# Where the product that spreads a norm's factor stands in three feed-forward layers

## The reference, cut to what matters

```python
D_FF = 2816

def rms_norm_2(x, g, eps=NORM_EPS):
    x32 = x.astype(jnp.float32)
    y = x32 * lax.rsqrt(jnp.mean(x32 * x32, axis=-1, keepdims=True) + eps)
    return (y * g.astype(jnp.float32)).astype(x.dtype)

def swiglu(h, w_gate, w_up, w_down):
    return (jax.nn.silu(h @ w_gate) * (h @ w_up)) @ w_down

for layer in range(DEPTH):          # DEPTH = 2
    x = x + 0.5 * swiglu(rms_norm_2(x, ffn_norm[layer, 0]), ...)
    ...                             # attention mixer, or RWKV time mixing
    x = x + 0.5 * swiglu(rms_norm_2(x, ffn_norm[layer, 1]), ...)
```

## Time and profile before

| | |
|---|---|
| median of 3 runs | 2799.5 us (2792.75 to 2800.39) |
| the profiled execution's own time | 2794.96 us |
| its span, from the first to the last instruction | 2793.2 us |
| mean granted TensorE clock | 0.947 |
| busy share of TensorE, DVE, ACT, POOL | 86%, 67%, 43%, 23% |
| spreading products start at (layers 1 to 4) | 1641.4, 1952.8, 2144.1, 2612.1 us |

### The profile page before, as it was taken

One profiled execution on the slowest core, in us unless ns is written; L12 is line 12 of the kernel. 1 busy time (PEld: TensorE's weight loads), 2 busy tenths in 40 slices (PEclk: granted clock), 3 DMA queues, 4 the chain that ended last, 5 costly groups with the idle time before them and its releaser, 6 DMA issues. The chain is left out here.

```text
span 2793.2 us, 35053 instructions
## 1 busy us (share of the span) xinstructions
PE 2397.1 (86%) x12802; PEld 1590.6 (57%) x12802; DVE 1861.0 (67%) x3446; ACT 1206.1 (43%) x2554; POOL 638.9 (23%) x530
## 2 busy tenths in 40 slices
PE   6987788888778887888888879998999997976999
PEld 5664333333224443433332268898888886865887
DVE  4667766677656757777765566676666665778665
ACT  3433434444335443444434354456445443534443
POOL 0003434554344433455544300000000000010000
PEclk8999999999999998999999999999999998966999
DMA  9789999999999888999999935542554554212553
GB/s 379 261 344 395 403 425 423 425 427 423 427 426 359 358 369 363 423 427 427 427 423 427 397 128 189 182 150 110 178 191 168 187 189 141 82 48 94 179 180 120
DMA packets 124203, 815.14 MB, mean 292 GB/s; under 512 B 15539, under 2 KB 20699, under 8 KB 29340
## 3 DMA queue, kind: packets, MB, share of 16 engines
q0 software_dynamic: 74016, 539.00, 46.2%
q1 hardware_dynamic: 50044, 274.27, 27.2%
HBM read 811.02 MB, written 1.15 MB: 291 GB/s over the span
## 5 line engine op out<-in xcount | busy, mean ns | idle before, releaser
L1372 PE MATMUL bank<-rows,diag 128*128 128x512 f32 (+1 forms) x2056 | 1018.3, 630 | 249.5 <-ACT diag L1522 246.6
L1754 DVE CUSTOM_DVE_ANT_0 rows<-rows,h 128x1024 f32<-128x1024 f32 (+1 forms) x512 | 622.3, 1225 | 399.4 <-DMA rows<-in_peer_rows,idx 395.9
L1372 PEld LDWEIGHTS bank<-rows,diag 128*128 128x128 f32 (+1 forms) x2056 | 374.6, 197 | 800.5 <-ACT diag L1522 482.1
L1259 POOL DMA_INDIRECT rows<-in_peer_rows,idx x512 | 618.9, 1209 | 777.2 <-PE bank L1372 651.4
L2091 PE MATMUL bank<-hT_pair,high 128*128 128x512 f32 x1408 | 503.2, 401 | 12.5 <-DVE work L2195 4.2
L2028 DVE TENSOR_TENSOR low<-weight_ring,high 128x2048 fp32r<-128x2048 f32 x148 | 338.4, 2289 | 164.8 <-ACT high L2023 164.8
L1513 ACT ACTIVATE picks<-picks 128x1 f32<-128x1 f32 (+1 forms) x512 | 103.4, 202 | 714.8 <-DVE picks L1754 710.2
L2092 PE MATMUL bank<-hT_pair,low 128*128 128x256 f32 x1408 | 396.1, 281 | 0.0
L2023 ACT CAST high<-weight_ring 128x2048 fp32r<-128x2048 f32 x148 | 281.8, 1908 | 147.7 <-PE bank L2100 115.8
L2091 PEld LDWEIGHTS bank<-hT_pair,high 128*128 128x128 f32 x1408 | 266.2, 189 | 81.0 <-issue 6.6
L2092 PEld LDWEIGHTS bank<-hT_pair,low 128*128 128x128 f32 x1408 | 267.5, 190 | 1.7
(11 more groups left out here) (540 smaller groups left out, 3265.5 us busy)
## 6 DMA issues: line engine op xcount, KB each, us to landing
weight_ring<-in_ffn_w_gate SPq DMA_DIRECT2D x44, 1024.0 KB, 4.8
weight_ring<-in_ffn_w_up SPq DMA_DIRECT2D x44, 1024.0 KB, 4.9
weight_ring<-in_ffn_w_down SPq DMA_DIRECT2D x44, 1024.0 KB, 4.8
mod_ring<-in_mod_w SPq DMA_DIRECT2D x16, 1024.0 KB, 7.1
weight_ring<-in_peer_w_q SPq DMA_DIRECT2D x16, 1024.0 KB, 12.2
half_ring<-in_mod_w SPq DMA_DIRECT2D x24, 512.0 KB, 7.9
rows<-in_mod_w SPq DMA_DIRECT2D x12, 1024.0 KB, 10.1
weight_ring<-in_attn_w_in SPq DMA_DIRECT2D x12, 1024.0 KB, 4.9
```

Of the source, the lines that this page charges most:

```text
L1259: nc.gpsimd.indirect_dma_start(ring[:, s], None, dram["peer_rows"], bass.IndirectOffsetOnAxis(ap=idx[:, T, n:n + 1], axis=0)).then_inc(row ...
L1372: mm = nc.tensor.matmul(bank[:, :], diag[0:n, j % DIAG_SLOTS], ring[0:n, j % ROW_SLOTS, D + half * 512:D + (half + 1) * 512], start=(j in ...
L1754: dotted.up(nc.vector.tensor_tensor_reduce(out=ring[r, s, 0:D], in0=ring[r, s, 0:D], in1=its_h, scale=1.0, scalar=0.0, op0=ALU.mult, op1=A ...
```

## The change

In the three layers whose first banks are the upper ones, TensorE goes on to piece 1's gate product right after piece 0, then makes the spreading product, then piece 1's up product. Piece 1's gate product no longer waits for a join, since banks 0 and 1 hold nothing then. The second layer stays as it was. No instruction is added on any engine.

```diff
@@ __init__
+        self.apart = not set(first_banks) & set(range(4))
@@ up_products
-    def up_products(self, pe, f, reg=None, late=None):
+    def up_products(self, pe, f, reg=None, late=None, which=(0, 1)):
-        for v in range(2):
+        for v in which:
             b = self.up_block(f, v)
             self.wait(pe, self.split.sem, self.p0 + b + 1, reg, 6)
-            if f > 0:
+            if f > 1 or f == 1 and (v == 1 or not self.apart):
                 self.wait(pe, self.steps.sem, self.m0 + 4 * (f - 1) + v + 1, reg, 8)
@@ multiply
+        def spread_factors():
+            pe.wait_ge(self.placed.sem, self.pl0 + 1)
+            for T in range(NT):
+                mm = nc.tensor.matmul(kit.bank[self.spread_bank][:, T * P:(T + 1) * P], kit.ones[:, 0:P], self.halves.spread[:, T, :],
+                                      start=True, stop=True)
+            mm.then_inc(self.spread.sem, 1)
+
         self.up_products(pe, 0, late=late)
-        pe.wait_ge(self.placed.sem, self.pl0 + 1)
-        ...
-        for f in (1, 2):
-            self.up_products(pe, f)
-            self.down_products(pe, f - 1)
+        if self.apart:
+            self.up_products(pe, 1, which=(0,))
+            spread_factors()
+            self.up_products(pe, 1, which=(1,))
+        else:
+            spread_factors()
+            self.up_products(pe, 1)
+        self.down_products(pe, 0)
+        self.up_products(pe, 2)
+        self.down_products(pe, 1)
```

More of the change, by code:

```diff
@@ L2114, in multiply @@
         kit, nc = self.kit, self.kit.nc
-        self.up_products(pe, 0, late=late)
-        pe.wait_ge(self.placed.sem, self.pl0 + 1)
[L2117 to L2120, removed]
-        for f in (1, 2):
-            self.up_products(pe, f)
-            self.down_products(pe, f - 1)
+        def spread_factors():
[4 more added lines that the diff above has]
+            mm.then_inc(self.spread.sem, 1)
+        self.up_products(pe, 0, late=late)
+        if self.apart:
[8 more added lines that the diff above has]
+        self.down_products(pe, 1)
         with pe.Fori(0, self.loops - 1) as i:
```

## The result

| | before | changed |
|---|---|---|
| median | 2792.82 us (6 runs) | 2813.77 us (6 runs, 2810.57 to 2816.11) |
| ratio | | 1.0068, 95% interval 1.0058 to 1.0078 |
| profiled execution, span | 2793.2 us | 2808.8 us |
| gate and up products wait for DVE L2028: total, times, longest | 4.2 us, 4, 1.2 | 26.8 us, 5, 8.2 |

The change costs 0.68%: 19.0 us on 2793, with an interval of 16.2 to 21.8 us. I had predicted 2817 us in a range of 2808 to 2824. The medians lie 21 us apart; the ratio, taken over all runs, gives less, since two of the six runs of the kernel before came out near 2800. The 25 and 23 further runs of the kernel before that were taken beside the experiments have medians of 2795.4 and 2795.45 us, 18 us under the changed kernel's.

The account below looks back on a forecast made before the run. TensorE was taken to bound the steady part, leaving only the layers' openings open to the change; 5.65 + 5.65 + 2.5 + 6.0 = 19.8 us on a mean of 2796.9 us gave 2817 us, range 2808 to 2824 us.

Parts of the forecast that it names:

- The chain is rigid: Fourth layer: the 8.13 us from the factor's copy to block 3's low part move whole with the later spreading product.
- Fourth and third layer +5.65 us each, first layer +2.5 us: Before piece 1's up: 16 gate pairs put ahead cost 5.65 us; in the first layer they partly fill the 2.66 us factor wait.
- Second layer 0: Opening of the second layer: order unchanged, so 0 us.
- The clock, 2.0 us a layer, 6.0 in all: Piece 1's up in three layers: slow pairs after 8.3 us of new idle time, 2.0 us each.
- its bounds of 4.2 and 9.6: Ends of the clock term over three layers: 3 x 1.4 = 4.2 us and 3 x 3.2 = 9.6 us.
- The lower row: First layer's gate of piece 1 before the change: five pairs take 3.23 us against 1.84, a loss of 1.4 us.
- leaving the term out: Sum without the slow clock, 13.8 us; as the rival where the clock stays up, 2811 us, 14%.
- The margin behind it: Piece 2's gate, waiting for block 5's split: 2.8 us of margin remain, so nothing more is lost or won back.
- The sum: Whole kernel: 5.65 + 5.65 + 2.5 + 6.0 = 19.8 us, added to a mean of 2796.9 us, predicting 2817 us.
- The faster rival: Piece 1's gate: idle time is filled and nothing comes late, 8.3 us won, time 2789 us; 2%.

Follow-up runs that it names:

- no_join_wait: Kernel before, with only the join's wait before piece 1's gate dropped in three layers, the spreading product staying ahead of that gate; ratio 1.0002 (0.9987 to 1.0017).
- early_block: Changed kernel, with block 3 (piece 1's up weights) split before piece 0 is treated, in all four layers; ratio 1.0029 (1.0018 to 1.0039).
- half_gate: Changed kernel, with the spreading product in the middle of piece 1's gate, behind 8 of its 16 pairs; ratio 1.0053 (1.0035 to 1.0072).

## Why the prediction was right

By its own steps:

- *The chain is rigid, 8.13 us from the copy to the split block.* Right to the hundredth in the changed kernel, and right in the three that moved or filled what lies beside it: the up follows 8.81 us behind the spreading product in the third and fourth layer as long as the block is in the chain, 8.80 to 8.92 in the first.
- *Fourth and third layer +5.65 us each, first layer +2.5 us.* From the transposes to piece 1's up the trace shows +5.4 (2635.04 - 2610.09 against 2620.95 - 2601.37), +5.8 and +2.4 us, 13.6 in all against 13.8. The gate's 16 pairs took 5.55 us in the fourth layer where I had 5.65.
- *Second layer 0.* -0.08 us.
- *The clock, 2.0 us a layer, 6.0 in all.* Somewhat too much. The ledger leaves 18.3 - 13.6 + 0.1 = 4.8 us for it, 1.6 us a layer, and the kernel with TensorE kept busy gives 4.5. This is the one term of the sum that was mis-sized, and it lies within its bounds of 4.2 and 9.6. The lower row, the first layer's 1.4 us, was the nearer one. I had chosen 2.0 us by the length of the idle time and the pauses behind it. Other waits show that the price does not follow that length (last section), so that 2.0 came near is in part luck. Against leaving the term out, the kernel that was kept busy decides: the 4.5 us are there, a quarter of the loss. The section on the clock gate in the Trainium skill's page "TensorE: Matmul & The Clock Gate" says only that the ramp costs under 1% of a typical kernel and that a count of cold matmuls is not to be fitted; leaving the term out was my reading of it. Its figure agrees with this case, 4.5 of 2793 us being 0.16%; it is the change that is small as well.
- *The margin behind it.* Right. No new wait in the changed kernel, none even where the block was moved ahead.
- *The sum.* 19.8 us predicted; 18.3 by the ledger, 19.0 by the ratio. The forecast of 2817 us lies 3 us above the median, partly by the clock and partly because I added the sum to a mean of four executions, 2796.9 us, two of which were high. How much falls to each depends on the base: the 48 later runs of the kernel before have medians near 2795.4 us, which makes about 1.5 us each, while on the first six runs' median of 2792.82 the sum alone would have ended 1 us too low.
- *The faster rival* needed the chain behind the copy to be no longer than what stands beside it. As printed it could not be. Taken apart in the experiments, its mechanism does exist: with block 3 out of the way, the dropped wait and the filled factor wait both pay.

## What to carry to other kernels

When a product only starts a chain on other engines, and TensorE waits at the end of that chain, independent work belongs behind the product, beside the chain, and not ahead of it: here, what was put ahead was paid in full, less the time that the product's own input was still missing. Two short waits in a timeline say little about which of them matters; follow the one that ends the longer chain back to its start, and look at what else is in that chain for no reason of data. Here that was a weight split: taking it out, with the product placed layer by layer, won 0.4% where filling the visible idle time lost 0.7%.

## What the runs showed of the hardware that I had not expected

The price of a slow clock did not grow steadily with the idle time before it. This is what piece 1's up took over and above the 5.65 us of its 16 pairs at the full clock, for each wait that the traces show:

| idle time before piece 1's up | lost, us (layer) |
|---|---|
| 2.6 to 2.7 us (no_join_wait) | 1.3 (1), 0.1 (3), 1.6 (4) |
| 4.2 us (early_block) | 2.1 (1), 1.5 (3), 1.4 (4) |
| 5.4 us (half_gate) | 2.9 (1), 1.5 (3), 2.7 (4) |
| 8.2 us (changed) | 1.6 (1), 1.7 (3), 1.5 (4) |

So waits of one length within one execution differed by up to 1.5 us, the shorter wait of the half gate was in two of three layers dearer than the longest, and the 0 to 1.6 us a layer that I had allowed it was too narrow. The pace of the pairs shows the two levels directly: 0.64 us a pair at 1.2 GHz and 0.35 at 2.4, with five slow pairs behind the fourth layer's wait of 8.21 us and nine behind that of 5.42. What decides between these cases was not tried, and each figure is from one execution.
